# Cross attention of a decoder step: the samples' rows and the last prompt tile's values in another place

## What is computed

```python
def memory_cross_attention(h, mk, mv, lp):
    q = (h @ lp['w_cq']).reshape(B, T, X_HEADS, X_HEAD)                  # 4 heads x 128
    s = jnp.einsum('bthd,bshd->bhts', q, mk) * (X_HEAD ** -0.5)
    pr = jax.nn.softmax(s, axis=-1)
    o = jnp.einsum('bhts,bshd->bthd', pr, mv).reshape(B, T, X_WIDTH)
    return o @ lp['w_co']
# x = x + memory_cross_attention(rms_norm(x), mk, mv, lp), then x = x + hierarchical_moe(rms_norm(x), lp)
```

## Time and profile before

| | |
|---|---|
| runs | 803.42, 804.76, 805.93 us; median 804.76 us |
| profiled execution | 802.58 us, span 800.7 us |
| PE busy | 699.5 us (87% of the span) |
| DVE, ACT, POOL busy | 355.3, 218.9, 92.3 us |
| mean granted TensorE clock | 0.912 of full speed |
| cross attention on PE, first query product to last router product | 488.9 to 617.9 us |

### The profile page before, as it was taken

How to read it: one execution, slowest core, us unless ns; L and a number is a source line. 1 busy time by engine, 2 the same in 40 slices (tenths; PEclk the granted TensorE clock), 3 DMA queues, 4 the chain that set the end, 5 groups by cost and what they waited for, 6 DMA issues and landing times.

```text
span 800.7 us, 16356 instructions
## 1 busy us (share of the span) xinstructions
PE 699.5 (87%) x7084; PEld 531.3 (66%) x7084; DVE 355.3 (44%) x734; ACT 218.9 (27%) x544; POOL 92.3 (12%) x122
## 2 busy tenths in 40 slices
PE   4999999899997989989999998998797279999933
PEld 3884788778887888877956446765346257777711
DVE  4210027996146577466552222445525832222217
ACT  4250113432332222244621011422312012222214
POOL 0100000000276400000000000000000034444210
PEclk9899999999999999995798998996987579999976
DMA  9732313000210100022223703022629669999735
GB/s 313 267 106 86 125 32 126 1 0 1 61 64 4 56 5 4 3 62 71 96 106 89 289 1 106 13 67 80 236 81 396 260 222 408 406 406 405 294 117 228
DMA packets 42493, 113.91 MB, mean 142 GB/s; under 512 B 10187, under 2 KB 12677, under 8 KB 41116
## 3 DMA queue, kind: packets, MB, share of 16 engines
q1 hardware_dynamic: 36964, 102.18, 34.8%
q0 software_dynamic: 4864, 8.53, 2.9%
q10 hardware_dynamic: 592, 2.13, 0.7%
HBM read 105.88 MB, written 16.24 MB: 153 GB/s over the span
## 4 chain that ended last, share of the span: by engine, by line
PE 78%; DVE 13%; DMA 3%; ACT 2%; issue 2%; SPq 0%; POOLq 0%; DVEq 0%
PE bank L905 58%; PE bank L1574 7%; PE bank L909 5%; PE bank L1588 4%; PE bank L1560 3%; DVE arena L2009 1%; PE bank L1582 1%; DMA arena<-pair_d 1%; DMA arena<-in_norm_mix 1%; DVE arena L2146 1%; DVE arena L2473 1%; DMA arena<-hn_d,arena 1%; ACT arena L1767 1%; DMA pair_d<-arena 0%; DVE arena L2465 0%
## 5 line engine op out<-in xcount | busy, mean ns | idle before, releaser
L905 PE MATMUL bank<-arena 64*64 64x64 f32 (+12 forms) x5284 | 529.3, 296 | 54.2 <-DMA arena<-pair_d 11.3
L905 PEld LDWEIGHTS bank<-arena 64*64 64x64 f32 (+5 forms) x5284 | 395.8, 158 | 176.5 <-issue 107.5
L909 PE MATMUL bank<-arena 128*128 128x128 f32 (+5 forms) x392 | 55.8, 293 | 23.7 <-DMA arena<-in_norm_mix 10.4
L909 PEld LDWEIGHTS bank<-arena 128*128 128x128 f32 (+5 forms) x392 | 48.9, 164 | 36.7 <-DMA arena<-in_norm_mix 10.4
L1574 PEld LDWEIGHTS bank<-arena 128*64 128x64 f32 x1024 | 57.5, 136 | 19.8 <-issue 19.8
L1574 PE MATMUL bank<-arena 128*64 128x128 f32 x1024 | 62.4, 273 | 0.0
L861 POOL DMA_INDIRECT arena<-hn_d,arena x16 | 16.7, 1043 | 393.4 <-DVE arena L2412 372.8
L2433 DVE TENSOR_TENSOR arena<-bank,arena 128x512 f32<-128x512 f32 x32 | 22.2, 692 | 54.0 <-PE bank L1560 54.0
L1679 ACT COPY arena<-bank 128x260 f32<-128x260 f32 x40 | 15.0, 375 | 109.9 <-PE bank L905 109.9
L1783 ACT COPY arena<-bank 128x256 f32<-128x256 f32 x56 | 20.8, 372 | 66.8 <-PE bank L905 65.3
L865 POOL DMA_INDIRECT pair_d<-arena x32 | 31.8, 993 | 60.2 <-ACT arena L1892 53.2
(11 more groups left out here) (241 smaller groups left out, 538.0 us busy)
## 6 DMA issues: line engine op xcount, KB each, us to landing
arena<-in_w_exp_gate SPq DMA_DIRECT2D x32, 512.0 KB, 11.0
arena<-in_w_exp_up SPq DMA_DIRECT2D x32, 512.0 KB, 13.0
arena<-in_w_exp_down SPq DMA_DIRECT2D x32, 512.0 KB, 14.1
arena<-in_w_in SPq DMA_DIRECT2D x5, 2048.0 KB, 9.2
arena<-in_x_prompt SPq DMA_DIRECT2D x8, 512.0 KB, 6.2
arena<-in_w_out SPq DMA_DIRECT2D x2, 2048.0 KB, 7.9
arena<-in_cache_mem_k SPq DMA_DIRECT2D x8, 512.0 KB, 7.5
arena<-in_cache_mem_v SPq DMA_DIRECT2D x8, 512.0 KB, 3.7
```

Source lines behind the costliest of these rows:

```text
L905: last[0] = pe.matmul(out, lhsT, rhs, start=start, stop=stop, skip_group_check=True)
L909: last[0] = pe.transpose(out, in_, ident[0:n, 0:n])
```

## The change

Two tables change, and with them what follows from them. In `CROSS_ORDER` the samples' rows `qb` stand closer together and earlier among the query projections, so that more of them come ahead of the last projections; the values of the first tile, `("xp", 0)`, stand ahead of `("q", 1, 0)` instead of behind it; and the values of the last tile, `("xp", 3)`, are gone from the table. They are a step `"xp3"` of `WC_ORDER` now, behind the output product of tile 0. PE's wait ahead of `WC_ORDER` is for the third tile alone, and the product of tile 1 waits for the last one. SP's first two expert loads wait for the last tile's value products (`("xo", 3)`) instead of `("qb", 7)`, since they overwrite what these read.

```diff
 CROSS_ORDER = tuple(("q", h, 1) for h in range(4)) + (
-    ("qrow", 0), ("xs", 0), ("q", 0, 0), ("xs", 1), ("xn", 0), ("qb", 0), ("q", 1, 0), ("xp", 0), ("xn", 1),
-    ("qb", 1), ("q", 2, 0), ("xp", 1), ("qb", 2), ("q", 3, 0), ("xs", 2), ("qb", 3), ("xs", 3), ("xn", 2), ("qb", 4),
-    ("xp", 2), ("xn", 3), ("qb", 5), ("xp", 3), ("qb", 6), ("qb", 7))
+    ("qrow", 0), ("xs", 0), ("q", 0, 0), ("xs", 1), ("xn", 0), ("qb", 0), ("xp", 0), ("qb", 1), ("q", 1, 0), ("xn", 1),
+    ("qb", 2), ("xp", 1), ("qb", 3), ("q", 2, 0), ("qb", 4), ("q", 3, 0), ("xs", 2), ("qb", 5), ("xs", 3), ("xn", 2),
+    ("qb", 6), ("xp", 2), ("xn", 3), ("qb", 7))
-WC_ORDER = (0, "csT", 1, "cpT", "co", 2, "coT", 3, 4)
+WC_ORDER = (0, "xp3", "csT", 1, "cpT", "co", 2, "coT", 3, 4)
...
# bank_plan
+        elif step == "xp3":
+            g += [(("xpT", 3, i), "a") for i in range(2)] + [(("xo", 3), "a")]
...
# SP
-            sp.wait_ge(full, place[("qb", 7)] + 1)
+            sp.wait_ge(full, place[("xo", 3)] + 1)
             for i in range(2):
                 load_expert(i, i, s_wgu[i], s_wd[i])
...
# PE, cross_output(t)
+                elif t == 1:
+                    done(pe, ("xo", 3))
...
-            done(pe, ("xo", 3))
+            done(pe, ("xo", 2))
             weights_in(pe, ("w_co",))
             for step in WC_ORDER:
...
+                elif step == "xp3":
+                    prompt_values(3)
...
# ACT, loop over WC_ORDER (values_copied(n) holds the three copies of ("xp", n), unchanged)
+                elif step == "xp3":
+                    values_copied(3)
```

More of the change, by code:

```diff
@@ L1837, in _, with values_copied @@
                 row_norm("wo", t)
+            def values_copied(n):
+                for i in range(2):
+                    o = filled(act, ("xpT", n, i))
+                    act.copy(PTc[:, 2 * i:2 * i + 2, :, :], o[:, :].rearrange("p (n a q) -> p n a q", n=2, a=2)) \
+                        .then_inc(evac["a"], 1)
+                o = filled(act, ("xo", n))
+                t = CROSS_TILES[n]
+                act.copy(yT[:, 0:4, t * P:(t + 1) * P], o[:, :].rearrange("p (c q) -> p c q", c=4)) \
+                    .then_inc(evac["a"], 1)
             for what, n, *half in CROSS_ORDER:
@@ L1854, in _ @@
                 elif what == "xp":
[L1855 to L1862, removed]
+                    values_copied(n)
                 elif what == "qrow":
@@ L2321, in _ @@
                         ins.then_inc(evac["v"], 1)
-                elif step != "co":
+                elif step not in ("co", "xp3"):
                     residual("wc", 5, 3, "xT3", step)
```

## The result

The changed kernel takes 809.57 us (median of 20 executions, 801.47 to 814.96), the kernel before 803.39 in as many on the same chips (791.72 to 806.69). The ratio of the two is **1.0099** (95% interval 1.0068 to 1.013), which is +8.0 us on 803.39. The ratio, here and in the table of the experiments, leaves out executions over 1.5% above the fastest of their kernel, which are 9 of 20 before and 3 of 20 changed here and up to half of those of the kernel before there, so the distance of the medians of all executions, here **+6.2 us**, is given beside it. The means of all lie 6.3 us apart, with 2.4 us either way as two standard errors. The forecast was slower, by 8.4 us.

The account below looks back on a forecast made before the run. PE's program was taken to bound the kernel, through its waits and lower clock. Waits of +4.9 us and clock of +3.5 made +8.4; on the profiled 802.58 us or a median 2.2 higher, 812.5 us was predicted, range 807 to 817.5.

Parts of the forecast that it names:

- The first wait: Ahead of the first tile's transposes PE would stand for DVE's normalise: 1.4 us, bounds 1.2 and 1.7.
- The 2.46 and the 4.17 us stay: PE's waits ahead of the third tile's transposes and the samples' turned weights would not change.
- The last values' wait: Ahead of the last tile's value products PE would wait 3.75 us on ACT's copies instead of 0.67: +3.1 us.
- Ahead of tile 1's product: PE would wait about 0.45 us for the copy of the last values, partly covered by csT.
- Expert loads: SP would issue the first two experts' loads some 9 us later, at cost 0.
- The first fall: Clock falls around the first tile's values: 4.5 us at 6 in 10, counted as +2.7 us.
- The fall at the last values: A new clock fall around the last tile's values, nearly sure: +2.8 us.
- The third tile's gain: Behind the third tile's values the clock would rise 3 to 7 us sooner: -2.0 us, bounds 1.5 to 3.4 gained.
- The clock's sum: Clock changes at the first, last and third tile's values together: +3.5 us.
- waits only: Rival: no first fall, and the earlier rise pays for the second; 4.9 + 0 to 1 us, about 809; chance 0.22.
- Dearer clock: Rival: both new falls come, the first for 6.2 us, the third tile gains nothing: +13.9, about 817.5 us; chance 0.17.
- Not slower: Rival: the third tile's low-clock stretch goes (-6.2 us) and no new one appears: -1.3 us, about 803.5; chance 0.08.

Follow-up runs that it names:

- e2: Kernel before with only the first tile's values moved ahead of the second query projection; ratio 1.0058 to the kernel before, medians +1.7 us.
- e4: Changed kernel with ACT copying the last tile's turned probabilities ahead of tile 0's row norm; ratio 1.0094 to the kernel before, medians +1.8 us.
- e3: Kernel before with only the last tile's values moved behind tile 0's output product; ratio 1.0107 to the kernel before, medians +3.8 us.
- e1: Changed kernel with first and last tile's values back in their old places, only the samples' rows denser; timed twice, ratios 1.0036 and 0.9981 to the kernel before.
- e8: Changed kernel with unread products filling its two new waits; ratio 1.0057 to the kernel before, medians +2.5 us.
- e9: Kernel before with unread products filling three of its old waits; ratio 0.9909 to the kernel before, medians -8.9 us.
- e7: Kernel before with the samples' softmax early on DVE and three samples' rows ahead of the third tile's values; median 786.99 us, ratio 0.9832.

## Why the prediction was right

By its own steps:

- *The first wait.* Predicted 1.4 us (1.2 to 1.7), measured 1.35 in the change and alone in e2. DVE's row ends at 509.04 + 1.23 = 510.27, the transposes start at 510.32. Right.
- *The 2.46 and the 4.17 us stay.* 2.47 and 4.18. Right.
- *The last values' wait.* Predicted 3.75 us, measured 3.65; +3.0 for the +3.1 of the sum. e4 shows that the row norm on ACT makes it.
- *Ahead of tile 1's product.* Predicted 0.45 us, measured 0.25, and 0.46 in e3. At the lower clock `csT` takes longer (0.63 us for 0.38) and covers more of the copy.
- *Denser rows cost nothing.* Right, by the waits of e1 and two ratios about 1.
- *Expert loads.* SP issues them at 568.76, 85.3 us behind the first query product where it was 75.5, so 9.8 us later for the 9 predicted, and PE still waits for no weights. Right.
- *The waits' sum.* +4.9 predicted, +4.6 measured.
- *The first fall.* It came, at 511.4 for 10.3 us. Busy 9.57 us of it cost half, 4.8; the term had 4.5, weighted by 0.6 to 2.7. In e2 (6.8 us) and e4 (10.4) it came too.
- *The fall at the last values.* It came, but for 3.4 us: 3.25/2 = 1.6 us instead of 2.8. In e3 it did not come, so "nearly sure" was too strong. Tile 1's wide products ran at full speed from 569.5.
- *The third tile's gain.* 5.07/2 = 2.5 us for 6.2 is a gain of 3.6 us, where -2.0 was taken from bounds that ended at 3.4.
- *The clock's sum.* +3.5 predicted. The three stretches give 4.8 + 1.6 - 3.6 = +2.8, the fall at `cpT` costs 2.3 for 2.8, and PE's busy time says +2.8. e8 gives 4 to 5 us from its own execution. The sign and size hold, but the terms were 2.1 us too low at the first fall and 1.2, 1.6 and 0.5 too high at the three others; that they cancelled to within about 1 us is luck. The parts are not worth their decimals: each changes with the execution.

The rivals: *waits only* (+4.9 us, a ratio of about 1.006) lies just below the interval of the ratio, from 1.0068, but within 2.4 us of the 6.3 by which the means of all executions differ; so the changed kernel's time alone does not rule it out. What speaks against it are e9's whole time, which fell though the filling brings no data sooner, and e8's stage. *Dearer clock* failed, since the stretches at the last values and at the third tile were short, although the first was long. *Not slower* had its mechanism right (the third tile's fall was halved, 3.6 us) and not its size against the rest. That the table load drains ACT, which the Trainium skill states (ScalarE: Activation LUTs, "What ACT_TABLE_LOAD costs"), this trace does not show either: 562.85 + 1.28 = 564.13, and the root starts at 564.15. By the warning against long idle gaps, which the Trainium skill gives (TensorE: Matmul & The Clock Gate, "Why this matters for your kernels"), the first fall would not have come. The trace does not agree: behind the wait of 1.35 us the clock fell at 511.4, and it did not fall there once e8 had filled it.

What stays open: how often each fall comes, and with it how much of the change's cost is the clock. Each program has one profile (e1 has two), and e1 to e4 differ by up to 4.6 us in PE's busy time for the same instructions. By the medians the change costs 6.2 us, of which the waits are 4.6.

## What to carry to other kernels

Where PE walks a fixed order and bounds the kernel, moving work pays only by what it does to PE's waits, so write down for each moved step when its operand is ready and what the producing engine does just ahead of it: three copies behind a row norm with a table load cost 3 us here. Count a wait twice, once by its length and once by half of PE's busy time in the low-clock stretch behind it (in e7 the clock was 7.6 of the 13.4 us gained). Look for work that is ready to stand in the longest waits first; unread products are the second choice, and they must be counted at the lower clock's length.

## What the runs showed of the hardware

- The clock fell at the end of eight transposes (1.10 us) that followed 1.35 us of waiting, and stayed down for 10.3 us although PE was busy for 9.57 of them. It fell behind the same wait in e2 (for 6.8 us) and in e4 (for 10.4), and with 1.06 us of the wait filled it stayed up (e8, one profile).
- The same instructions on the same data ran with the clock down at other places from one execution to the next. Up to the cross attention, where the two kernels don't differ, PE was busy for 450.2 us in the one and 443.8 in the other. With it goes a spread of up to 2% between executions, and intervals of about half a per cent from 12 of them.
- A row norm's square root starts 0.02 us behind its table load, in both kernels.
